# Two transformer blocks on one core: the second block's projections start with the context tokens, in three split passes

## The reference

```python
x = rms_norm(x, final_g)                       # end of the first block
hx = _modulate(_rmsnorm(x, norm1_g), sh1, sc1)     # xn * (1 + scale) + shift
hc = _modulate(_rmsnorm(ctx, norm1_g), csh1, csc1)
qa, ka, va, qr, kr, vr, gr = split(hx @ w_in)      # w_in: 1024 x 2304
_,  ka_c, va_c, _, kr_c, vr_c, _ = split(hc @ w_in)
# head norms and rotary positions on q, k; softmax attention over context + own keys;
# retention (decay-weighted, both directions, started from the context's state); group norm * silu(gr)
x_new = x + gt1 * (concat([attn_x, ret_x]) @ w_out)
h2 = _modulate(_rmsnorm(x_new, norm2_g), sh2, sc2)
# router: top group of 4, top 2 of its 8 experts; 32 SwiGLU experts 1024 -> 512 -> 1024
x = _rmsnorm(x_new + gt2 * moe(h2), final_norm_g)
```

## Time and profile before

| | |
|---|---|
| three runs | 2081.47, 2082.81, 2091.58 us |
| profiled execution | 2081.88 us, span 2080.1 us |
| feed-forward, mixes of the first block | 0 to 1349.5 us |
| norms of the second block | 1349.5 to 1378 us |
| 13 products | 1378 to 1477 us |
| attention, retention, `w_out2`, router | 1477 to 1594 us |
| experts and output | 1594 to 2080 us |

### The profile page before, as it was taken

One profiled execution on the slowest core, in us unless ns is written; L12 is line 12 of the kernel. 1 busy time (PEld: TensorE's weight loads), 2 busy tenths in 40 slices (PEclk: granted clock), 3 DMA queues, 4 the chain that ended last, 5 costly groups with the idle time before them and its releaser, 6 DMA issues.

```text
span 2080.1 us, 33242 instructions
## 1 busy us (share of the span) xinstructions
PE 1984.5 (95%) x13991; PEld 1629.1 (78%) x13991; DVE 1132.3 (54%) x1939; ACT 655.0 (31%) x980; POOL 0.2 (0%) x4
## 2 busy tenths in 40 slices
PE   7999999998999999999999999979997998989997
PEld 7999998887999999999888999968665444434443
DVE  6665669845655665666984556554475222222222
ACT  4433436614333533343661433320332000000001
POOL 0000000000000000000000000000000000000000
PEclk9999999999999999999999999999899999999999
DMA  7798553448776677655244877612305999999995
GB/s 223 246 356 244 170 172 95 132 132 233 223 220 194 205 220 215 196 170 173 92 132 135 260 222 214 166 41 81 142 23 203 421 422 420 422 420 422 421 421 246
DMA packets 273950, 475.56 MB, mean 229 GB/s; under 512 B 28182, under 2 KB 234064, under 8 KB 249224
## 3 DMA queue, kind: packets, MB, share of 16 engines
q1 hardware_dynamic: 267148, 471.75, 65.8%
q10 hardware_dynamic: 6652, 1.65, 0.6%
HBM read 472.22 MB, written 7.95 MB: 231 GB/s over the span
## 4 chain that ended last, share of the span: by engine, by line
PE 78%; DMA 16%; DVE 3%; ACT 1%; ACTq 1%; issue 0%; SPq 0%; DVEq 0%
PE ps L692 77%; DMA ring_zone<-in_moe_w_up_dram 16%; PE ps L992 1%; ACTq L395 1%; PE ps L1128 0%; DVE hl L1706 0%; DVE xT L1713 0%; DVE WL L1695 0%; DMA PT<-in_norm_g_dram 0%; SPq L618 0%; ACT WH L1370 0%; DVE xT L1758 0%; ACT gT L1501 0%; DVE xT L1889 0%; DVE h2l L2266 0%
## 5 line engine op out<-in xcount | busy, mean ns | idle before, releaser
L1695 DVE TENSOR_TENSOR WL<-W,WH 128x1024 fp32r<-128x1024 f32 x372 | 452.3, 1223 | 324.7 <-ACT WH L1370 324.3
L692 PE MATMUL ps<-hh,WH 128*128 128x256 f32 x2128 | 604.7, 284 | 18.8 <-DVE WL L1695 13.1
L692 PE MATMUL ps<-hl,WH 128*128 128x256 f32 x2128 | 595.8, 280 | 0.0
L692 PE MATMUL ps<-hh,WL 128*128 128x256 f32 x2128 | 595.4, 280 | 0.0
L1370 ACT ACTIVATE WH<-W 128x1024 fp32r<-128x1024 f32 x372 | 391.0, 1056 | 469.1 <-PE ps L692 429.0
L692 PEld LDWEIGHTS ps<-hh,WH 128*128 128x128 f32 x2128 | 401.8, 189 | 32.5 <-issue 21.1
L692 PEld LDWEIGHTS ps<-hl,WH 128*128 128x128 f32 x2128 | 401.9, 189 | 0.2
L692 PEld LDWEIGHTS ps<-hh,WL 128*128 128x128 f32 x2128 | 401.6, 189 | 0.0
L692 PE MATMUL ps<-ring_over,XT 128*64 128x512 f32 x896 | 228.2, 594 | 31.0 <-DMA ring_zone<-in_moe_w_up_dram 14.3
L692 PEld LDWEIGHTS ps<-ring_over,XT 128*64 128x64 f32 x896 | 77.1, 137 | 176.1 <-issue 176.0
L692 PE MATMUL ps<-hid_h,WH 128*128 128x256 f32 x704 | 200.5, 285 | 0.0
(11 more groups left out here) (330 smaller groups left out, 2194.9 us busy)
## 6 DMA issues: line engine op xcount, KB each, us to landing
ring_over<-in_moe_w_gate_dram SPq DMA_DIRECT2D x64, 1024.0 KB, 20.4
ring_zone<-in_moe_w_down_dram SPq DMA_DIRECT2D x64, 1024.0 KB, 18.8
ring_over<-in_moe_w_up_dram SPq DMA_DIRECT2D x48, 1024.0 KB, 22.5
W<-in_ffn_w_gate_dram SPq DMA_DIRECT2D x88, 512.0 KB, 4.9
W<-in_ffn_w_up_dram SPq DMA_DIRECT2D x88, 512.0 KB, 4.4
W<-in_ffn_w_down_dram SPq DMA_DIRECT2D x88, 512.0 KB, 3.9
W<-in_w_in_dram SPq DMA_DIRECT2D x78, 512.0 KB, 4.4
W<-in_w_gate_dram SPq DMA_DIRECT2D x48, 512.0 KB, 3.7
```

The lines of the kernel that those rows point to most:

```text
L692: ins = nc.tensor.matmul(o, lhsT, rhs, start=start, stop=stop, skip_group_check=True, **kw)
L1695: v.tensor_tensor(low, W[:, i % RAW, :], high.bitcast(F32), ALU.subtract).then_inc(low_ready, 1)
```

## The change

`w_in2` joins the split weights. The 13 products are put in the order 3, 6, 2, 5, 8, 7, 0, 1, 4, 11, 12, 10, 9, so that two products of the context come first; chunks of `w_in2` are loaded in the order of their first use. The context is normed, turned and modulated in blocks 5 to 7 of the last feed-forward stage, where its high and low parts are made too, and the router's row with it. The two norms of x are joined: with s the mean square of x and s_g that of `x * final_g`, the modulated input is `x * final_g * (1 + scale) * norm1_g / sqrt(s_g + EPS * (s + EPS))` plus the shift. ACT squares both x and `x * final_g`; both sums are made in one bank, between the halves of the first product. `final_g` is applied to the residual later (after the sixth product), and the decay matrix of head 0 is made after the eleventh.

```diff
+ORDER = (3, 6, 2, 5, 8, 7, 0, 1, 4, 11, 12, 10, 9)
+CHUNK = {0: 0, 1: 1, 2: 2, 3: 2, 4: 3, 5: 4, 6: 4, 7: 5, 8: 5, 9: 6, 10: 6, 11: 7, 12: 8}
+SIDE = {1: [("ss", 3)], 3: [("ss", 2)], 4: [("rot", 2)], 5: [("rot", 5)], 7: [("ss", 0)], 8: [("ss", 1), ("rot", 0)],
+        9: [("rot", 1)], 10: [("rot", 4)]}
+CONTEXT_AT = 5
+RESIDUAL_AT, DECAY_AT = 5, 10
-SPLIT = ("ffn_gate", "ffn_up", "ffn_down", "w_in", "w_gate")
+SPLIT = ("ffn_gate", "ffn_up", "ffn_down", "w_in", "w_gate", "w_in2")
...
# PE, ffn(1, 1)
+                    if (l, i, b) == (1, 1, CONTEXT_AT + 1):
+                        turn_context()
...
# PE, the products
-                            mm(bank[:, f * T:(f + 1) * T], w[:, j * 256 + f * P:j * 256 + (f + 1) * P], src[:, k, :],
-                               k + f == 0, end, then=work_ready if end and f else None)
+                        mm3(bank[:, f * T:(f + 1) * T], at(w, j * 256 + f * P), (src[0][:, k, :], src[1][:, k, :]),
+                            k + f == 0, end, then=work_ready if end and f else None)
...
+            for p, g in enumerate(ORDER):
+                product(held[c], bank, g, 0)
+                if p == 0:
+                    block_sums(sums)
+                product(held[c], bank, g, 1)
+                if p == CHUNK_LAST[c]:
+                    done_pair(2)
+                if p == 0:
+                    mm(bank[:, 0:T], ones[:, :], rs[:, :], True, False)
+                    mm(bank[:, T:2 * T], ones[:, :], rstd[:, :], False, True, then=work_ready)
+                for kind, piece in SIDE.get(p, []):
+                    side(kind, piece)
...
# ACT
+            def round_modulated():
+                for k in range(KD):
+                    act.wait_ge(h_plain, due(h_plain))
+                    nc.scalar.activation(hh[:, k, :], nT[:, k, :], ACT.Identity, bias=MOD[:, k, 0:1])\
+                        .then_inc(norm_h, 1)
...
+                if p == 0:
+                    block_roots()
+                    round_modulated()
+                if g < 4:
+                    square(g)
...
+                if p >= 2 and p == CHUNK_LAST[CHUNK[g]]:
+                    split_to(min(st["split"] + 2, len(split_at)))
...
# DVE
+                for k in range(KD + 1):
+                    if k < KD:
+                        v.scalar_tensor_tensor(out=nT[:, k, :], in0=xT[:, k, :], scalar=G1[:, 0, k:k + 1],
+                                               in1=rstd[:, :], op0=ALU.mult, op1=ALU.mult).then_inc(h_plain, 1)
+                    if k:
+                        dve.wait_ge(norm_h, due(norm_h))
+                        v.scalar_tensor_tensor(out=hl[:, k - 1, :], in0=nT[:, k - 1, :], scalar=MOD[:, k - 1, 0:1],
+                                               in1=hh[:, k - 1, :].bitcast(F32), op0=ALU.add, op1=ALU.subtract)\
+                            .then_inc(h_ready, 1)
...
+                if p == 0:
+                    modulated()
+                for kind, piece in SIDE.get(p, []):
+                    side(kind, piece)
+                if p >= 2 and p == CHUNK_LAST[CHUNK[g]]:
+                    split_to(min(st["split"] + 2, len(split_at)))
+                if p == RESIDUAL_AT:
+                    normed_residual()
+                if p == DECAY_AT:
+                    decay_arg(0)
+                    decay_sum(0)
```

More of the change, by code:

```diff
@@ L210, in stream_plan @@
         ffn((l, 1))
-    for c in range(9):
+    for c in sorted(CHUNK_FIRST, key=CHUNK_FIRST.get):
         add("w_in2", 0, c)
@@ L1023, in _ @@
                 ffn(l, 1)
[L1025 to L1035, removed]
@@ new lines, in _, with product @@
+            idx = {}
+            high_of, low_of = {True: hc_h, False: hh}, {True: hc_l, False: hl}
+            def product(ws, bank, g, half):
+                of_context = g in OF_CONTEXT
+                w = ws[half]
+                src = high_of[of_context], low_of[of_context]
+                for j in range(4):
+                    k = 4 * half + j
+                    end = k == KD - 1
+                    if g == 2:
+                        pe.wait_ge(h_ready, due(h_ready))
+                    rows = [0, 1] if g not in (2, 3, 7, 8, 9, 10) else [0] if g in (2, 3) else []
+                    for f in rows:
+                        mm3(bank[:, f * T:(f + 1) * T], at(w, j * 256 + f * P), (src[0][:, k, :], src[1][:, k, :]),
+                            k + f == 0, end, then=work_ready if end and f else None)
+                    if g in (2, 3, 7, 8, 9, 10):
+                        n, v0 = (P, T) if g in (2, 3) else (256, 0)
+                        for tt in range(TT):
+                            part = [a[:, k, tt * P:(tt + 1) * P] for a in src]
+                            mm3(bank[:, v0 + tt * n:v0 + (tt + 1) * n], part, at(w, j * 256 + 256 - n, n),
+                                k + tt == 0 and not rows, end, then=work_ready if end and tt else None)
@@ L1401, in root, with split_to @@
                     .then_inc(rms, 1)
-            def norm(src, last=False, rs_free=0):
+            def split_to(n):
+                while st["split"] < n:
+                    i = split_at[st["split"]]
+                    act.wait_ge(raw_loaded[i % RAW], 16 * (i // RAW + 1))
+                    high, _, before = split_place(st["split"])
+                    act.wait_ge(pair_used, before + 1)
+                    nc.scalar.activation(high, W[:, i % RAW, :], ACT.Copy).then_inc(high_ready, 1)
+                    st["split"] += 1
@@ L1407, in norm @@
[L1407 to L1414, removed]
-                turns.step()
+                    for k in (2 * b, 2 * b + 1):
+                        nc.scalar.activation(nT[:, k, :], xT[:, k, :], ACT.Square, scale=col("final_g", k))
@@ L1518, in _ @@
                 ffn(l, 1)
[L1521 to L1525, removed]
+            block_squares()
+            split_to(in2_at + 4)
             def evac_wait(n):
@@ L1543, in side @@
                 turns.step()
[L1545 to L1557, removed]
             def decay(h):
@@ L1567, in decay @@
                 nc.scalar.activation(own, own, ACT.Exp).then_inc(dexp, 1)
-            decay(0)
+            for p, g in enumerate(ORDER):
+                if g >= 11:
+                    bank = look()
+                    nc.scalar.activation(S[:, TANH_AT[g], :], bank[:, 0:512], ACT.Tanh, scale=0.5)\
+                        .then_inc(gate_ready, 1)
+                idx[g] = turns.step()
+                if p == 0:
[8 more added lines that the diff above has]
+                if p == DECAY_AT:
+                    decay(0)
             for s in range(19):
@@ L2015, in _ @@
                         update(b, 0.5)
[L2018 to L2047 removed]
+            block_sums()
+            split_to(in2_at + 4)
             def both(dst, swapped, src):
```

287 lines of the change are left out of this document (169 added, 118 removed).

## The result

The changed kernel takes 2070.49 us, the median of five runs (2068.35 to 2071.15), against 2082.91 of the kernel before beside it: ratio 0.993, 95% interval 0.9912 to 0.9948. It is faster by 12.4 us. I had forecast 2056.6 in a range of 2047 to 2068, so the sign is right, the time lies above the range, and less than half of the 26.2 us came. The profiled execution took 2069.35, its span is 2067.4; before it was 2081.88 and 2080.1, so the traces account for 12.7 us.

The account below looks back on a forecast made before the run. PE carries 78% of the chain, DMA 16%, in three stages with three limits. Products 26.1 plus into attention 5.0 minus feed-forward 4.9 gives 26.2 us saved; 2082.8 - 26.2 = 2056.6 us, with 80% in 2047 to 2068.

Parts of the forecast that it names:

- Charged: 4.9: Feed-forward blocks 5 to 7: turns, router's row, waits for DVE and ACT's context squares add 4.9 us.
- I charge 2: Ahead of product 2: PE stands 5.1 us for a square by ACT; the 1.2 GHz clock behind it costs 2 us.
- Call 1349.5 the end: Start mark of the head: the last feed-forward product was taken to end at 1349.5 us.
- The rest of the products, 67.5: Behind product 2: ten products 56.0 us, sides 6.0, PE's waits for DVE 5.5, ending at 1451.2.
- Products 5.6 and 8.2: Split products cost 5.6 us each, products 2 and 3 8.2 each, against 6.84 plain: 10.9 us saved.
- into attention: From last product to first row maximum: 1.2 us instead of 6.2, the decay being made under products; 5.0 saved.
- one for one at the end: Expert stage: what the second block's front saves makes the expert stream start and end earlier by the same time.
- Rival 1: DVE paces the products: 8 us more waits, 4 more in decay and feed-forward; 14 us gained, 2069; chance 0.17.

Follow-up runs that it names:

- after_ss: The changed kernel with the sum of squares of piece 3 behind product 2 instead of ahead of it: 2055.7 us, ratio 0.9865 to the kernel before.
- after_5: The changed kernel with the products' order starting 6, 3, 5, 2, so product 5 follows the wait instead of product 2: 2063.93 us, ratio 0.9907.
- after_0: The changed kernel with `eps_sq` in the second word of the tile of `eps`, so no address behind it moves: 2063.71 us, ratio 0.9906.
- before_32: The kernel before with one unused 4-byte tile where the change allocates `eps_sq`, nothing else: 2091.58 us against 2083.75, ratio 1.0041.
- after_0_ss: The changed kernel with `eps_sq` in the tile of `eps` and the sum of squares of piece 3 behind product 2: 2052.32 us, ratio 0.9846.

## Why the prediction missed

- **The feed-forward stage, "Charged: 4.9".** The parts that I worked out held: 4.4 for the turns and the row, no wait on WL behind them. (In the traces of after_ss and after_5, with the same code there, they took 6.0, with the clock at 0.50 for 3.4 us behind them.) What failed was a step that isn't there: I took the time of untouched code as given. The tile `eps_sq` stood in the diff. Of the 5.7 us by 1268.35, 0.7 is there at the first evacuation. after_0, which has no shift, is 0.9 of the other 5.1 late too, so the shift cost 4.2 by this place; what the 0.9 is stays open.
- **The head, "I charge 2" for the clock.** This is the largest mis-sized term: 9.3 measured. The place of the wait and the level of the clock were right; the duration came from the earlier trace rows, behind which other passes ran. Product 2 took 7.4 us more than at full clock, product 5 1.9. after_ss shows that wait and clock together cost 13.1 us. The wait itself was 1.5 shorter than forecast, and PE's restart came 1383.45 - 1361.97 = 21.5 us behind the last feed-forward pass instead of 23.5.
- **"Call 1349.5 the end".** DVE's first update is no mark of PE's end, which came 1.9 us later.
- **The rest of the products, 67.5.** It took 70.1 from product 2's end to the last. PE waits 3.5 where I had 5.5; against that stand 1.9 for product 5 at the low clock, some 0.5 for the slower passes (0.9% of 56 us) and some 1.7 for the 3.4 us of low clock behind the last wait on WL, which I had not priced. The remaining half us is not taken apart.
- **Products 5.6 and 8.2, into attention, one for one at the end**: right. Product 2 at full clock took 8.1 (1381.26 to 1389.37 in after_ss).

The 13.7 us by which the maximum came later than forecast are then 5.7 for the feed-forward stage, 1.9 for the mark, 3.5 up to product 2's end (37.75 instead of 34.2: 5.4 more in product 2, 2.0 less ahead of it) and 2.6 behind it. Rival 1, DVE as the pace, came nearest in time (2069), by chance, and was the wrong mechanism: taking DVE's burst away gains 3.5 us up to attention, not 12, and of these 1.2 are waits.

By the Trainium skill ("SBUF — State Buffer", "SBUF: two separate sides") PE never waits for another engine or a transfer on SBUF's engine side, and its rule on where an operand starts ("Operand start alignment") is about what is legal, not about speed. No wait of that kind is in the rows here. The pace of the passes depends on the place of their tiles all the same, as the table shows.

By the Trainium skill ("TensorE: Matmul & The Clock Gate", "Part 1: The HAM clock gate") the clock has two levels, as here (0.50 and 1.00), and what it takes to come back is a matter of time and not of the matmuls issued. Measured from PE's restart were 3.1 us in after_5, 4.1 in the kernel before, 17.8 in after_0 and 20.3 in the changed kernel, with PE busy in all, so here one time does not describe it; the measurement decides.

## What to carry to other kernels

Compare the pace of untouched code in the two traces before looking at the change: a 4-byte tile that moves the operands of the hot loop cost 4 to 8 us (4.2 by the trace of after_0, 7.8 by the median of before_32) where the change gained 12.4, and packing it into a tile beside it won it back. Price a wait of PE with the clock behind it, and look at which passes run there: 3.6 us became 13, and moving one short instruction group behind the next product removed all of it. Take the end of an engine's stage from its own timeline, not from the engine that follows.

## What the runs showed of the hardware that I had not expected

- Split passes of 256 columns take 0.117 us each (5.60/48) or 0.120 (5.76/48) by where their tiles lie, in steps of 32 bytes, at the same granted clock and without a wait in the profile. What collides is not shown.
- Busy PE stayed at the low clock for 20.3 us in the changed kernel and 17.1 in after_0, both times through all of product 2 with its passes of 128 columns.
- Whether the clock falls behind a short wait differs between executions: behind the same 2.15 us on WL it was low for 3.4 us in the changed kernel and in after_0_ss, and not at all in after_0. A difference of 2 us between two traces can be this alone.
